# Router products with the turned rows as stationary operand, context transposes moved behind them, first weights in three pieces behind products of ones

## The reference, cut to what matters

```python
logit_g = xt @ w_group + b_group          # 4 groups
g_sel = argmax(logit_g)
logit_e = (xt @ w_router + b_router)      # 16 experts, 4 in the group that was picked
top_v, top_i = top_k(softmax(logit_e of g_sel), 2)
y = sum over the two experts: weight * (silu(xt @ w_gate) * (xt @ w_up)) @ w_down
```

## Time and profile before

| | |
|---|---|
| time, median of 3 runs | 917.15 us (916.23 to 917.5) |
| the profiled execution's own time | 916.66 us |
| its span (first to last instruction) | 914.9 us |
| TensorE products busy | 893.6 us, 98% |
| VectorE, ScalarE, GpSimd busy | 364.2, 214.2, 165.1 us |
| DMA | 188.47 MB, mean 206 GB/s |

### The profile page before, as it was taken

The page is one execution under the profiler, slowest core; times in us unless marked ns, Lnnn a source line. Parts: engine busy times, 40 slices in busy tenths (PEclk is TensorE's granted clock), DMA queues, the critical chain, the costliest instruction groups (busy, mean ns, idle before and its releaser), DMA issues.

```text
span 914.9 us, 13380 instructions
## 1 busy us (share of the span) xinstructions
PE 893.6 (98%) x5548; PEld 519.0 (57%) x5548; DVE 364.2 (40%) x802; ACT 214.2 (23%) x468; POOL 165.1 (18%) x159
## 2 busy tenths in 40 slices
PE   7999999999999989999999999999999999999998
PEld 3588875456565436444334333344688888856653
DVE  1764543457755453210210210047635542444331
ACT  2211213344545210010110110124202111633320
POOL 3212220000003054230230200033202213260000
PEclk9999999999999999999999999999999999999999
DMA  9935549124011968999999999961382102700002
GB/s 328 316 111 184 185 169 393 59 93 184 1 47 37 296 193 321 401 414 429 422 420 428 421 427 430 400 228 47 110 172 101 45 9 81 241 1 2 1 12 80
DMA packets 71454, 188.47 MB, mean 206 GB/s; under 512 B 31185, under 2 KB 31841, under 8 KB 65121
## 3 DMA queue, kind: packets, MB, share of 16 engines
q1 hardware_dynamic: 62416, 162.41, 48.2%
q0 software_dynamic: 5488, 18.37, 5.4%
q10 hardware_dynamic: 3488, 6.82, 1.9%
HBM read 168.70 MB, written 18.89 MB: 205 GB/s over the span
## 4 chain that ended last, share of the span: by engine, by line
PE 89%; DVE 4%; DMA 2%; ACT 2%; POOL 2%; issue 1%; SPq 0%; DVEq 0%; ACTq 0%; POOLq 0%
PE psum L944 20%; PE psum L1138 18%; PE psum L1159 9%; PE psum L1045 6%; PE psum L866 6%; PE psum L1290 5%; PE psum L970 5%; PE psum L993 4%; PE psum L1007 2%; PE psum L1024 2%; PE psum L1361 2%; PE psum L1072 2%; PE psum L1251 2%; POOL qk_st L2531 1%; PE psum L907 1%
## 5 line engine op out<-in xcount | busy, mean ns | idle before, releaser
L1138 PE MATMUL psum<-ring,buf_a 128*32 128x512 f32 x1536 | 168.6, 592 | 3.1 <-issue 3.0
L1138 PEld LDWEIGHTS psum<-ring,buf_a 128*32 128x32 f32 x1536 | 67.1, 110 | 100.9 <-issue 90.9
L1159 PE MATMUL psum<-ring,buf_c 128*32 128x512 f32 x768 | 86.0, 593 | 0.5 <-issue 0.4
L2604 POOL DMA_INDIRECT buf_b<-xq_d,o_sb x48 | 51.8, 1078 | 159.5 <-DVE buf_a L2220 129.5
L2243 DVE TENSOR_TENSOR buf_c<-buf_c,psum 128x512 f32<-128x512 f32 x12 | 13.0, 1086 | 155.7 <-PE psum L1138 155.7
L2531 POOL TENSOR_TENSOR qk_st<-qk_st,half 128x8 f32<-128x8 f32 x26 | 43.6, 1678 | 158.3 <-DVE qk_st L2302 72.9
L944 PE MATMUL psum<-ring,buf_a 128*128 128x256 f32 x320 | 70.9, 380 | 0.0
L944 PE MATMUL psum<-ring,buf_b 128*128 128x256 f32 x288 | 64.8, 380 | 0.0
L944 PEld LDWEIGHTS psum<-ring,buf_a 128*128 128x128 f32 x320 | 60.1, 190 | 8.2 <-issue 0.4
L1870 DVE TENSOR_TENSOR s_buf<-s_buf,psum 128x512 f32<-128x512 f32 x52 | 35.3, 685 | 61.2 <-PE psum L944 57.8
L1045 PE MATMUL psum<-ring,buf_b 128*128 128x512 f32 x128 | 58.2, 593 | 0.0
(11 more groups left out here) (307 smaller groups left out, 1160.5 us busy)
## 6 DMA issues: line engine op xcount, KB each, us to landing
ring<-in_moe_w_gate SPq DMA_DIRECT2D x16, 2048.0 KB, 12.4
ring<-in_moe_w_up SPq DMA_DIRECT2D x16, 2048.0 KB, 13.5
ring<-in_moe_w_down SPq DMA_DIRECT2D x16, 2048.0 KB, 15.1
ring<-in_w_in SPq DMA_DIRECT2D x7, 2048.0 KB, 14.7
ring<-in_w_ada SPq DMA_DIRECT2D x6, 2048.0 KB, 10.3
ring<-in_da_w_in SPq DMA_DIRECT2D x5, 2048.0 KB, 21.1
y_d<-ring POOLq DMA_DIRECT2D x1, 5632.0 KB, 21.7
y_d<-buf_b ACTq DMA_DIRECT2D x11, 512.0 KB, 11.0
```

What stands on the lines that cost most here:

```text
L1138: last = mm(buf("mm", n)[rows, :], x_part[:, j, k, :], slot(moe_load(q, m, r))[:, k, :], start=(k == 0), stop=(k == KD - 1))
L1159: last = mm(buf("sc", n)[rows, m, :], hidT[:, s % 3, f * P + SUB * j:f * P + SUB * (j + 1)], slot(moe_load(q, 2, r), FC)[:, f, m * CH:(m + ...
L2604: pool.indirect_dma_start(out=xg[:, s % 2, j * 256:(j + 1) * 256], out_offset=None, in_=xn_quarters, in_offset=bass.IndirectOffsetOnAxis(a ...
```

## The change

The first weights come in three pieces, blocks 0 and 1, 2 and 3, and 4 to 7, each with a semaphore of its own. TensorE does eight 128x128 products of ones by ones as soon as `ones` is filled, ahead of the first transposes, and three behind them; nothing reads their result. The context transposes and their copies leave the steps of the attention tail; TensorE does them in two pairs of sets around the gate row products, behind the router, and ScalarE copies two sets before the exponentials and two behind them. The router products take a 128x128 block of the turned rows as stationary operand and the 20 columns of `w_rt` as moving one, so the result is tokens by 20 and needs neither a copy nor transposes; tile 2 is split around the transposes of tile 3. The context's v products are done 2, 4 and 10 instead of 4, 4 and 8 at a time.

```diff
+FIRST_PARTS = [(0, 2), (2, 4), (4, 8)]
@@ tail_steps
-    if HEADS * TT + 7 <= s < HEADS * TT + 11:
-        todo.append(("cxT", s - HEADS * TT - 7))
@@ booking
-            elif name == "cxT":
-                book("tp", "cxT", m)
...
-    book("mm", "router_T")
+    for m in range(KD // 2):
+        book("tp", "cxT", m)
     book("mm", "router")
@@ SP
-                for b in range(2):
-                    ks = slice(4 * b, 4 * b + 4)
-                    sp.dma_start(ring[:, W_IN, :].rearrange("p (k n) -> p k n", k=KD)[:, ks, :],
-                                 w_in[:, ks, 0:CH]).then_inc(first_landed if b == 0 else w_landed[W_IN], 16)
+                for piece, (lo, hi) in enumerate(FIRST_PARTS):
+                    sp.dma_start(ring[:, W_IN, :].rearrange("p (k n) -> p k n", k=KD)[:, lo:hi, :],
+                                 w_in[:, lo:hi, 0:CH]).then_inc(first_landed[piece] if hi < KD else w_landed[W_IN], 16)
@@ TensorE, start
+        def keep_busy(times):
+
+            for _ in range(times):
+                mm(bank(0, 0, 6)[:, 0:P], ones[:], ones[:], start=True, stop=True)
+
+        pe.wait_ge(pool_done, 2)
+        keep_busy(8)
         pe.wait_ge(pool_consts, 1)
         h_transposes(0)
+        keep_busy(3)
@@
-                if i == 0 and k == 0:
-                    pe.wait_ge(first_landed, 16)
-                if i == 0 and k == 4:
-                    landed(W_IN)
+                for piece, (lo, hi) in enumerate(FIRST_PARTS):
+                    if i == 0 and k == lo and hi < KD:
+                        pe.wait_ge(first_landed[piece], 16)
+                    elif i == 0 and k == lo:
+                        landed(W_IN)
@@ TensorE, attention steps
-                elif name == "cxT":
-                    pe.wait_ge(cx_ready, CT)
-                    n = turn["tp", "cxT", m]
-                    claim(pe, "tp", n)
-                    transposes(n, [cx[:, t, k * P:(k + 1) * P] for k in (2 * m, 2 * m + 1) for t in range(CT)])
@@ TensorE, router
+        def cx_transposes(m):
+
+            n = turn["tp", "cxT", m]
+            claim(pe, "tp", n)
+            transposes(n, [cx[:, t, k * P:(k + 1) * P] for k in (2 * m, 2 * m + 1) for t in range(CT)])
+
+        n = turn["mm", "router"]
+
+        def router(t, lo, hi):
+
+            for k in range(lo, hi):
+                if t == 0:
+                    drained(pe, "tp", turn["tp", "xT2", k])
+                if t == TT - 1:
+                    drained(pe, "tp", turn["tp", "xT2_last", k // 4])
+                last = mm(buf("mm", n)[:, t * 20:(t + 1) * 20], xT2[:, k, t * P:(t + 1) * P], w_rt[:, k, :],
+                          start=(k == 0), stop=(k == KD - 1))
+            return last
+
         pe.wait_ge(w_rt_ready, 1)
-        n_r = turn["mm", "router_T"]
-        claim(pe, "mm", n_r)
-        for k in range(KD):
-            drained(pe, "tp", turn["tp", "xT2", k])
-            mm(buf("mm", n_r)[0:20, 0:LAST], w_rt[:, k, :], xT2[:, k, 0:LAST], start=(k == 0), stop=(k == KD - 1))
+        claim(pe, "mm", n)
+        for t in range(TT - 2):
+            router(t, 0, KD)
+        router(TT - 2, 0, KD // 2)
         pe.wait_ge(xs2_ready, TT)
         for b in range(2):
...
-        for k in range(KD):
-            drained(pe, "tp", turn["tp", "xT2_last", k // 4])
-            last = mm(buf("mm", n_r)[0:20, LAST:SEQ], w_rt[:, k, :], xT2[:, k, LAST:SEQ], start=(k == 0), stop=(k == KD - 1))
-        fill(last, "mm", n_r)
-        n = turn["mm", "router"]
-        claim(pe, "mm", n)
-        drained(pe, "mm", n_r)
-        for t in range(TT):
-            last = transpose(buf("mm", n)[:, t * 20:(t + 1) * 20], logit_T[:, t * P:(t + 1) * P], ident[0:20, 0:20])
-        fill(last, "mm", n)
-
+        router(TT - 2, KD // 2, KD)
+        fill(router(TT - 1, 0, KD), "mm", n)
+
+        pe.wait_ge(cx_ready, CT)
+        cx_transposes(0)
+        cx_transposes(1)
         pe.wait_ge(gate_ready, 1)
         for c in range(2):
             n = turn["mm", "g_x", c]
             claim(pe, "mm", n)
             fill(mm(buf("mm", n), ones[:], o_sb[:, c * 512:(c + 1) * 512], start=True, stop=True), "mm", n)
 
-        cv_products(0, 4)
+        cx_transposes(2)
+        cx_transposes(3)
+        cv_products(0, 2)
         n = turn["mm", "places"]
...
-        cv_products(4, 8)
+        cv_products(2, 6)
         n = turn["mm", "ids"]
...
-        cv_products(8, CT * KD)
+        cv_products(6, CT * KD)
@@ ScalarE, behind the copy of tile 3's turned rows (the cxT branch of the attention steps is gone)
-        n = turn["mm", "router_T"]
-        filled(act, "mm", n)
-        drain(S.copy(logit_T, buf("mm", n)[0:20, :]), "mm", n)
+        act.wait_ge(mod_ready, 1)
+        cx_copies(0)
+        cx_copies(1)
         act.wait_ge(ge_in, 1)
         S.activation(g_exp[:], g_exp[:], ACT.Exp).then_inc(ge_out, 1)
         act.wait_ge(ge_in, 2)
         S.activation(in_group[:], in_group[:], ACT.Exp).then_inc(ge_out, 1)
+        cx_copies(2)
+        cx_copies(3)
```

More of the change, by code:

```diff
@@ L351, in build @@
     sel = sel_pad[:, TT:2 * TT, :]
-    logit_T = pT[0:20, 0, :]
     last_pick = o_sb[:, 0:512]
@@ L587, in build @@
     gain_loaded = sem("gain_loaded")
-    first_landed = sem("first_landed")
+    first_landed = [sem(f"first_landed{i}") for i in range(len(FIRST_PARTS) - 1)]
     early_loaded, late_loaded = sem("early_loaded"), sem("late_loaded")
@@ L1067, in cv_products @@
                 pe.wait_ge(cv_w_landed, 16)
-                drained(pe, "tp", turn["tp", "cxT", 2])
-                drained(pe, "tp", turn["tp", "cxT", 3])
             for piece in range(lo, hi):
                 t, k = divmod(piece, KD)
+                if t == 0 and k % 2 == 0:
+                    drained(pe, "tp", turn["tp", "cxT", k // 2])
                 last = mm(buf("sc", n)[:, t, :], cxT[:, k, t * P:(t + 1) * P], ring[:, 1, k * 512:(k + 1) * 512],
@@ L1075, in cv_products @@
                 fill(last, "sc", n)
[L1077 to L1082 removed]
+        def cx_transposes(m):
[12 more added lines that the diff above has]
+            return last
+        pe.wait_ge(w_rt_ready, 1)
+        claim(pe, "mm", n)
+        for t in range(TT - 2):
+            router(t, 0, KD)
+        router(TT - 2, 0, KD // 2)
         pe.wait_ge(xs2_ready, TT)
         for b in range(2):
[L1085 to L1097 removed]
+            n_x = turn["tp", "xT2_last", b]
+            claim(pe, "tp", n_x)
+            transposes(n_x, [xs2[:, TT - 1, k * P:(k + 1) * P] for k in range(4 * b, 4 * b + 4)])
+        router(TT - 2, KD // 2, KD)
[3 more added lines that the diff above has]
+        cx_transposes(1)
         pe.wait_ge(gate_ready, 1)
@@ L1544, in _ @@
                                      accum_out=cssq[:, 0, t:t + 1]).then_inc(c_ssq_ready, 1)
-                elif name == "cxT":
-                    act.wait_ge(mod_ready, 1)
-                    n = turn["tp", "cxT", m]
-                    filled(act, "tp", n)
-                    for kk in range(2):
-                        k = 2 * m + kk
-                        last = S.activation(cxT[:, k, :], buf("tp", n)[:, kk * CTX:(kk + 1) * CTX], ACT.Identity,
-                                            bias=mod_sh[:, 1, k:k + 1], scale=mod_g[:, 1, k:k + 1])
-                    drain(last, "tp", n)
                 elif name == "norm2_first":
@@ L1567, in _, with cx_copies @@
         drain(S.copy(xT2[:, 0:4, LAST:SEQ], buf("tp", n).rearrange("p (k n) -> p k n", k=4)), "tp", n)
-        n = turn["mm", "router_T"]
-        filled(act, "mm", n)
-        drain(S.copy(logit_T, buf("mm", n)[0:20, :]), "mm", n)
+        def cx_copies(m):
+            n = turn["tp", "cxT", m]
+            filled(act, "tp", n)
+            for kk in range(2):
+                k = 2 * m + kk
+                last = S.activation(cxT[:, k, :], buf("tp", n)[:, kk * CTX:(kk + 1) * CTX], ACT.Identity,
+                                    bias=mod_sh[:, 1, k:k + 1], scale=mod_g[:, 1, k:k + 1])
+            drain(last, "tp", n)
+        act.wait_ge(mod_ready, 1)
+        cx_copies(0)
+        cx_copies(1)
         act.wait_ge(ge_in, 1)
```

3 lines of the change are left out of this document (removed).

## The result

The changed kernel takes **918.25 us** (median of 20 runs, 916.34 to 921.77), the kernel before, run beside it, 917.03 us (20 runs). The ratio is 1.0019, with a 95% interval of 1.0011 to 1.0027: slightly slower, where 913.0 was forecast and 915.4 was the end of the range. The profiled execution took 919.04 us.

The account below looks back on a forecast made before the run. The prediction took TensorE, 89% of the chain of waits, to bound the kernel. Start 3.0, attention tail 0 and gather 1.1 summed to 4.1 us: profiled time 912.6, median 913.0, range 909.5 to 915.4.

Parts of the forecast that it names:

- Start, 3.0 us: At the kernel's start, ones and weights in pieces let products run sooner: gain 3.0 us, bounds 2.2 to 3.1.
- the estimate of 6.2: At the start: TensorE's clock rises at 6.2 us, some 5.0 us after the ones begin at 1.2.
- the clock isn't lifted: Rival at the start: the ones don't raise TensorE's clock, gain 0.7 instead of 3.0 us, time 915.3; chance 0.10.
- Attention tail, 0: End of attention: sixteen context transposes leave, 1.7 us of TensorE becomes idle time waiting for scaled rows; worth 0.
- Router at 0.11 per instruction: Router: 64 instructions at 0.11 us each, bounds 0.06 and 0.19; logits read at 312.2, 1.6 us sooner.
- a router over 8 us: Sign in the profile, at the router, that the forecast is wrong: the router lasts over 8 us.
- Four tenths given back by ScalarE's copies: Behind the router: four context copies ahead of the exponentials delay the second to 315.0, giving back 0.4 us.
- The gather waits for the stores: Rival between idx and gate: xq stores hold the gather, middle gain 0 to 0.3 us, time 914.1; chance 0.16.
- The load behind the context products at cost 0: Ahead of the second gate product: expert load issued 0.5 us later, landing near 343, wanted at 347.5; cost 0.
- The stall in the first gate product: Rival at the first gate product: its unexplained 3.4 us stall vanishes, gain 2.9 us more, time 910.0; chance 0.22.
- weight loads don't overlap: Rival at the router: kernel slower once each load exceeds 0.175 us; at 0.19, 1.0 us slower, 918.1; chance 0.03.
- 1.1 had been forecast as a gain: Router to gate: idx 1.2 us sooner, gather and gate taken as 1.1 sooner, bounds 0 and 1.2.

Follow-up runs that it names:

- e8: e4 with the xq stores of tiles 0 and 1 issued early and the expert load behind the context products held until set 0 is turned; 914.06 us, 0.9967.
- e10: e3 with the expert load behind the context products held until set 0's rows are turned; ratio 1.0002.
- e11: e3 with all 16 xq stores issued ahead of the up load and the load behind the context products held; 911.51 us, ratio 0.9969.
- e12: e4 with all 16 xq stores issued ahead of the up load and the load behind the context products held; 910.78 us, ratio 0.9970.
- e14: e1 with the expert load behind the context products held until set 0's rows are turned; 911.91 us, ratio 0.9975.
- e1: The kernel before with only the ones products and the first weights in three pieces added; 915.98 us, ratio 0.9991.
- e2: The changed kernel with the start of before (no ones, first weights in two halves); 921.88 us, ratio 1.0046.
- e3: The changed kernel with the 20 router columns streamed six times (120 columns moving), same weight loads; 922.97 us, ratio 1.0061.
- e4: The changed kernel with the router of before, context transposes still behind the router; 915.06 us, ratio 0.9972.
- e9: e10 with the xq stores of x tiles 0 and 1 issued ahead of the up load; ratio 0.9988.
- e5: The kernel before with the ones products alone, first weights in two halves as before; one run, 914.31 us.
- e13: The changed kernel with all 16 xq stores issued ahead of the up load and the load behind the context products held; 916.08 us, ratio 1.0030.

## Why the prediction was wrong

- **Start, 3.0 us: right.** 2.9 measured, with first products at 7.1 and the last half at 11.4. The clock is up at 5.3 in the changed kernel's profile; over all the profiles with the same ones it varies around the estimate of 6.2, from ahead of the transposes (e8, e10 and e11, whose eight take 1.04 to 1.06 us) to behind them (e12 and e14, 1.92 and 1.91, and fast products from 7.5). The rival "the clock isn't lifted" falls. The Trainium skill (TensorE: Matmul & The Clock Gate, Part 4) says that transposes don't count as activity; that they would therefore break the run of ones isn't borne out, since in e12 and e14 all eight ran slow and the clock still was up by 7.5. Whether they count isn't decided by these rows. One smaller step failed, without a price: the small vectors didn't land when they did before but 0.9 us later, ScalarE's Silu ran at 50.81 instead of 49.88, and VectorE's first block sum waited 1.08 us for ScalarE's copy, at 51.63, 0.2 later than 2.9 ahead. The next sum is 2.9 ahead again.
- **Attention tail, 0: right but for 0.4.** TensorE waits 1.19 us for the scaled rows at 291.24. The router starts 3.3 us sooner, of which 2.9 are the start's (e1); the other 0.4 come with the transposes that left (0.8 in e2 against the kernel before).
- **Router at 0.11 per instruction: the step that failed.** It holds for the first 40 instructions and then doubles, because the clock falls to 1.2 GHz. The prediction priced the new products by the places products, which run at 2.4 GHz and are ten instructions long, and carried that price over 64 narrow ones, the context transposes and the ones behind them. It looked for clock trouble at the start only; a fall in the middle was no rival and had no chance. Its sign of being wrong "a router over 8 us" came true: 10.7 us from 300.79 to the last product. The sum of what ran slow is 0.5 (tile 3's transposes, 1.57 against 1.09), 2.3 (24 instructions, 5.15 against e3's 2.84), 0.9 (transposes) and 1.3 (ones): 5.0 us, and places come 4.7 us later behind the router's start than in e3. With the clock kept (e3), logits come 8.2 us behind the router's start (8.1 forecast), idx 20.4 (20.7 forecast).
- **Four tenths given back by ScalarE's copies**: hidden under the fall, and too large. In e4, whose context copies stand in the same place, the second exponential runs 2.56 us behind the logits instead of 2.37, and places 5.82 instead of 5.62: 0.2. In e3 places come 5.67 behind, 0.05 more than before.
- **The gather waits for the stores**: this rival holds as soon as idx is early. e1, e3, e4, e9, e10 and e14 all wait for the stores, at 324.7 to 326.3; e5 and e8 don't, at 324.6 and 324.5. In the changed kernel idx was too late for it to show.
- **The load behind the context products at cost 0: wrong where it matters.** In the changed kernel it was issued at 334.63, past the gathers of set 0. With a router that keeps its clock it is issued at 330.1 and costs 5 us (e3 against e10). The Trainium skill (DMA: Bandwidth & Descriptors, Queues, rings and completion order) says that a DMA engine takes turns between the queues it has work for, packet by packet; e1's rows agree in so far as its gathers proceed under the load, but the fourth part is turned 11.2 us behind the gather's start (326.34 to 337.53); in e14, the same kernel with the load held, it is 6.7 (326.13 to 332.80).
- **The stall in the first gate product** stayed in the changed kernel (result at 345.19, 345.23 before), as the forecast had it.
- **The rival "weight loads don't overlap"** had the right sign and place and the wrong mechanism: it needed weight loads of over 0.175 each. The 24 last instructions do take 0.21, by the clock and not by the loads, as e3 shows with the same loads.

In sum: 4.1 us were forecast by the gate. The start brought 2.9 and the earlier router start 0.4 more, and from there to the gate 3.3 were lost where 1.1 had been forecast as a gain: 4.4 us in that one step. Behind the gate the profiled execution lost 2.4 more, where the forecast had expected nothing; at 919.04 it stands 0.8 above the median. The 20 runs' times follow their mean clock, so what parts them is mostly time at the lower clock; what the two waits behind the gate cost was not measured apart.

## What to carry to other kernels

A run of narrow products can be fully busy and still lose TensorE its clock, and the loss is paid by whatever stands behind them: read the granted clock over each new stretch, and cost it at both levels. A gain ahead of a gather counts only if the stores it reads and the next big load on the same queue keep step; otherwise it turns into idle time, behind which the granted clock fell in e1, e3, e9, e10 and e14. Here the start with the load held (e14) is worth 0.25%, and e8, e11 and e12 reach 0.3%; all four beat the kernel before and the changed one.

## What the runs showed that was not expected

- The granted clock fell to 0.50 with TensorE busy in 5.00 of 5.00 us, and not with products of 120 columns and the same weight loads. The Trainium skill (TensorE: Matmul & The Clock Gate, Part 1, HAM oscillation) describes such falls as driven by idle gaps of TensorE, above all waits for transfers. The idle time ahead of e1's and e3's gate agrees with it; the fall in the changed router has no such gap in front of it (TensorE is busy for 4.40 of the 4.40 us before 305.2).
- How long the clock stays down varies with the execution: 6.8 us (e13), 10.3 (changed) and 13.3 (e2) in the profiles.
- Streaming 120 columns instead of 20 behind a 128-column weight load is all but free: 4.62 against 4.54 us for 40.
- The stall in the first gate product (10.4 us for 64 instructions before, 10.4 in the changed kernel, 10.5 in e8) is gone in e11, e12 and e13: 7.1 us each. e8 and e12 have the same code on TensorE; only SP's order differs. So the place in TensorE's instructions doesn't decide it alone; the transfers around it do. That doesn't rule out the reading offered in the prediction, of an instruction fetch held up by dense transfers. What the product waits for stays open; no row names it. In e11 the product was read 8.0 us sooner and the kernel gained 2.8, so the 2.9 that the prediction gave this rival can't be told apart from the gate's own head start.
- The kernel before took 917.0 us (median of 20) in one series and 914.0 (of 31) in another, on another chip: 3 us, as much as most edits of this study. Whether the chip is the reason wasn't tried.
